# Cross attention with its heads spread between query tiles and output chunks, and one buffer of turned rows

## The reference

```python
def memory_cross_attention(h, m, wq, wkv, wo):
    q = (h @ wq).reshape(b, t, XA_HEADS, XA_HEAD_DIM)          # 4 heads of 256
    k, v = jnp.split(m @ wkv, 2, axis=-1)
    ...
    s = jnp.einsum("bthd,bmhd->bhtm", q, k).astype(jnp.float32) * (XA_HEAD_DIM ** -0.5)
    p = jax.nn.softmax(s, axis=-1).astype(v.dtype)
    o = jnp.einsum("bhtm,bmhd->bthd", p, v).reshape(b, t, D_MODEL)
    return o @ wo

# in each of the two layers l
x = x + memory_cross_attention(rmsnorm(x, norm_xa_g[l]), rmsnorm(mem, norm_mem_g[l]), xa_wq[l], xa_wkv[l], xa_wo[l])
x = x + conv_ffn_2(rmsnorm(x, norm_ffn_g[l]), ...)
```

## Time and profile before

| what | value |
| --- | --- |
| median of 3 runs | 2029.21 us |
| the profiled execution: its time, its span | 2029.21 us, 2027.3 us |
| mean granted TensorE clock | 0.996 |
| PE busy | 1992.5 us, 98% |
| POOL busy | 1444.9 us, 71% |
| DVE, ACT busy | 950.2 us, 614.2 us |
| chain that ended last, PE's share | 95% |
| cross attention of layer 0, from the first query tile to the end of the last output tile | 856.9 to 973.7 us |
| the same of layer 1 | 1537.6 to 1654.3 us |

### The profile page before, as it was taken

How to read it: one execution, slowest core, us unless ns; L and a number is a source line. 1 busy time by engine, 2 the same in 40 slices (tenths; PEclk the granted TensorE clock), 3 DMA queues, 4 the chain that set the end, 5 groups by cost and what they waited for, 6 DMA issues and landing times.

```text
span 2027.3 us, 25594 instructions
## 1 busy us (share of the span) xinstructions
PE 1992.5 (98%) x9432; PEld 1626.1 (80%) x9432; DVE 950.2 (47%) x1567; ACT 614.2 (30%) x1166; POOL 1444.9 (71%) x732
## 2 busy tenths in 40 slices
PE   8999989999999999999999999999999999999997
PEld 6787778888888888788888888877678888888886
DVE  4566444243444897555431422454655553233143
ACT  5554442221014344433210110236732321011011
POOL 7633379777877878874877778687578288777773
PEclk9999999999999999999999999999999999999999
DMA  5741233223223344331332223233013123233221
GB/s 170 138 65 63 81 102 115 94 97 101 94 88 110 104 156 156 104 94 42 96 102 94 95 93 104 76 99 115 1 46 101 42 94 104 94 95 103 94 86 60
DMA packets 57146, 190.79 MB, mean 94 GB/s; under 512 B 6288, under 2 KB 8080, under 8 KB 56944
## 3 DMA queue, kind: packets, MB, share of 16 engines
q1 hardware_dynamic: 52848, 182.71, 29.6%
q10 hardware_dynamic: 4192, 6.58, 1.1%
HBM read 183.50 MB, written 2.10 MB: 92 GB/s over the span
## 4 chain that ended last, share of the span: by engine, by line
PE 95%; DVE 2%; ACT 2%; issue 0%; DMA 0%; SPq 0%; POOL 0%; DVEq 0%; ACTq 0%
PE bank L713 29%; PE bank L715 29%; PE bank L714 29%; PE bank L1368 2%; PE bank L1047 1%; PE bank L958 1%; PE bank L1382 1%; PE bank L1398 1%; ACT EX L1920 1%; PE bank L773 0%; DVE PXL L2659 0%; DMA raw<-weights 0%; PE bank L1069 0%; PE bank L902 0%; DVE EX L2678 0%
## 5 line engine op out<-in xcount | busy, mean ns | idle before, releaser
L609 POOL TENSOR_TENSOR wH<-raw,zero 128x1024 fp32r<-128x1024 f32 (+1 forms) x303 | 577.6, 1906 | 396.0 <-PE bank L715 378.7
L612 POOL TENSOR_TENSOR wL<-raw,wH 128x1024 fp32r<-128x1024 f32 (+1 forms) x303 | 720.7, 2379 | 23.8
L713 PE MATMUL bank<-hnH,wH 128*128 128x512 f32 (+1 forms) x1456 | 575.2, 395 | 14.4 <-POOL wL L603 7.9
L714 PE MATMUL bank<-hnL,wH 128*128 128x512 f32 (+1 forms) x1456 | 569.0, 391 | 0.0
L715 PE MATMUL bank<-hnH,wL 128*128 128x512 f32 (+1 forms) x1456 | 568.9, 391 | 0.0
L713 PEld LDWEIGHTS bank<-hnH,wH 128*128 128x128 f32 (+1 forms) x1456 | 273.7, 188 | 78.4 <-issue 10.0
L714 PEld LDWEIGHTS bank<-hnL,wH 128*128 128x128 f32 (+1 forms) x1456 | 273.9, 188 | 58.4 <-issue 2.1
L715 PEld LDWEIGHTS bank<-hnH,wL 128*128 128x128 f32 (+1 forms) x1456 | 273.7, 188 | 58.5 <-issue 0.7
L713 PE MATMUL bank<-actH,wH 128*128 128x512 f32 x784 | 306.6, 391 | 0.0
L715 PE MATMUL bank<-actH,wL 128*128 128x512 f32 x784 | 305.4, 390 | 0.0
L714 PE MATMUL bank<-actL,wH 128*128 128x512 f32 x752 | 292.9, 390 | 0.0
(11 more groups left out here) (398 smaller groups left out, 2566.6 us busy)
## 6 DMA issues: line engine op xcount, KB each, us to landing
raw<-weights SPq DMA_DIRECT2D x315, 512.0 KB, 3.5
raw<-weights SPq DMA_DIRECT2D x28, 384.0 KB, 3.0
XT<-x_t SPq DMA_DIRECT2D x8, 256.0 KB, 6.4
XT<-x_t ACTq DMA_DIRECT2D x1, 2048.0 KB, 8.3
out<-MIX ACTq DMA_DIRECT2D x8, 256.0 KB, 2.2
maxB<-rowM SPq DMA_DIRECT2D x7, 256.0 KB, 16.5
qkO<-qkA SPq DMA_DIRECT2D x4, 256.0 KB, 4.1
memT<-mem_t ACTq DMA_DIRECT2D x1, 1024.0 KB, 5.6
```

Source lines behind the costliest of these rows:

```text
L609: nc.gpsimd.tensor_tensor(wH[:, slot, 0:w], raw[:, slot, 0:w], nothing.broadcast_to([P, w]), ALU.add)\
L612: nc.gpsimd.tensor_tensor(wL[:, slot, 0:w], raw[:, slot, 0:w], wH[:, slot, 0:w].bitcast(F32), ALU.subtract).then_inc(split, 1)
L713: mm(out_, aH, bH, start=first, stop=False)
L714: mm(out_, aH, bL, start=False, stop=False)
```

## The change

- PE: the attention no longer stands as a block between the two projections. Behind query tile 2 stands scores 0, behind tile 3 turn 0, behind tile 4 scores 1 and values 0, behind tile 5 turn 1, behind tile 6 scores 2 and values 1, behind tile 7 turn 2. Then come output tiles 0 and 1 with chunks 0 and 1; scores 3 and values 2; the same tiles with chunks 2 and 3; turn 3; chunks 4 and 5; values 3; output tile 2 with chunks 0 to 5; tiles 0 to 2 with chunks 6 and 7; tiles 3 to 7 one by one.
- ACT and DVE take their work in the same new order.
- The turned rows have one buffer in place of two, at another address, since the norm's output `hnH`, in whose memory they lay, is now still read. ACT waits for the value product of the head before.
- `OWN_BANKS` now holds banks for the row sum, the query tiles, the attention's tiles and the output tiles, in layer 1 those of layer 0 plus 5. Stages behind it that have no banks there continue from the last of them.

```diff
@@ the table of tiles and banks
-        TILES += [(f"row_sum_x{_i - 1}", 1), (f"xq{_i - 1}", 8), (f"xatt{_i - 1}", 24), (f"xo{_i - 1}", 8)]
+        _q, _a, _o = f"xq{_i - 1}", f"xatt{_i - 1}", f"xo{_i - 1}"
...
+        OWN_BANKS.update({_n: [(_b + (0, 5)[_i - 1]) % 8 for _b in _bs] for _n, _bs in (
+            (f"row_sum_x{_i - 1}", [0]), (_q, [1, 2, 3, 6, 1, 6, 1, 6]),
...
+            (_o, [1, 4, 5, 6, 7, 0, 2, 3]))})
@@ buffers
-        PXH = at("PXH", [P, 2, 2, S], F32R, offset=hn_at)
-        PXL = at("PXL", [P, 2, 2, S], F32R, offset=hn_at + 4 * KB2)
+        PXH = at("PXH", [P, 2, S], F32R, offset=up)
+        PXL = at("PXL", [P, 2, S], F32R, offset=up + 2 * KB2)
@@ PE, cross_attention
-                project(f"xq{l}", hnH, hnL, ready=lambda k: wait_hn(norm, k), lead=2,
-                        after={1: lambda: row_sums(TILE0[f"row_sum_x{l}"], norm)})
...
-                scores(0)
-                for h in range(3):
-                    scores(h + 1)
-                    turn(h)
-                    if h > 0:
-                        values(h - 1)
+
+                def output(tiles, chunks):
+
+                    for k in chunks:
+                        gone_wait(pe, xtile(base, "o", k // 2, k % 2))
+                        for i in tiles:
+                            u, n = POS[f"xo{l}", i], TILE0[f"xo{l}"] + i
+                            if k == 0:
+                                pe.wait_ge(split, u + 1)
+                                claim(n)
+                            cut = slice(k * P, k * P + P)
+                            last = three(psum(n)[:, :], wH[:, u % RING, cut], wL[:, u % RING, cut],
+                                         actH[:, k, :], actL[:, k, :], k == 0, k == KD - 1)
+                            if k == KD - 1:
+                                last.then_inc(unit_done, 1)
+
+                def scores_and_values(h):
+                    scores(h)
+                    values(h - 1)
+                project(f"xq{l}", hnH, hnL, ready=lambda k: wait_hn(norm, k), lead=2,
+                        after={1: lambda: row_sums(TILE0[f"row_sum_x{l}"], norm), 2: lambda: scores(0),
+                               3: lambda: turn(0), 4: lambda: scores_and_values(1), 5: lambda: turn(1),
+                               6: lambda: scores_and_values(2), 7: lambda: turn(2)})
+                output(range(2), range(0, 2))
+                scores_and_values(3)
+                output(range(2), range(2, 4))
                 turn(3)
-                values(2)
+                output(range(2), range(4, 6))
                 values(3)
-                project(f"xo{l}", actH, actL, ready=lambda k: gone_wait(pe, xtile(base, "o", k // 2, k % 2)), lead=2)
+                output(range(2, 3), range(0, 6))
+                output(range(3), range(6, KD))
+                for m in range(3, KD):
+                    output(range(m, m + 1), range(KD))
@@ ACT, rows
-                        if h >= 2:
-                            tile_wait(act, xtile(base, "o", h - 2, 1))
+                        if h >= 1:
+                            tile_wait(act, xtile(base, "o", h - 1, 1))
@@ ACT, the order (exponentials, rows and output_high keep their instructions)
+                for i in range(KD):
+                    query_high(i)
+                    if i in (2, 4, 6):
+                        exponentials(i // 2 - 1)
+                        if i > 2:
+                            output_high(i // 2 - 2)
+                    if i in (3, 5, 7):
+                        rows(i // 2 - 1)
+                exponentials(3)
+                output_high(2)
                 rows(3)
-                output_high(2)
                 output_high(3)
@@ DVE, the order (query, probabilities, rows_low and output_low keep their instructions)
+                for i in range(KD):
+                    query(i)
+                    if i in (2, 4, 6):
+                        probabilities(i // 2 - 1)
+                        if i > 2:
+                            output_low(i // 2 - 2)
+                    if i in (3, 5, 7):
+                        rows_low(i // 2 - 1)
+                memory_part(KD - 1)
+                probabilities(3)
+                output_low(2)
                 rows_low(3)
-                output_low(2)
                 output_low(3)
```

More of the change, by code:

```diff
@@ L181 @@
     if _i > 0:
-        TILES += [(f"row_sum_x{_i - 1}", 1), (f"xq{_i - 1}", 8), (f"xatt{_i - 1}", 24), (f"xo{_i - 1}", 8)]
+        _q, _a, _o = f"xq{_i - 1}", f"xatt{_i - 1}", f"xo{_i - 1}"
+        TILES += [(f"row_sum_x{_i - 1}", 1), (_q, (0, 1, 2)), (_a, (0, 1)), (_q, (3,)), (_a, (2, 3)), (_q, (4,)),
+                  (_a, (4, 5, 6, 7)), (_q, (5,)), (_a, (8, 9)), (_q, (6,)), (_a, (10, 11, 12, 13)), (_q, (7,)),
+                  (_a, (14, 15)), (_o, (0, 1)), (_a, range(16, 24)), (_o, range(2, 8))]
+        OWN_BANKS.update({_n: [(_b + (0, 5)[_i - 1]) % 8 for _b in _bs] for _n, _bs in (
+            (f"row_sum_x{_i - 1}", [0]), (_q, [1, 2, 3, 6, 1, 6, 1, 6]),
+            (_a, [4, 5, 7, 0, 2, 3, 4, 5, 7, 0, 2, 3, 4, 5, 7, 0, 2, 3, 5, 6, 7, 0, 2, 3]),
+            (_o, [1, 4, 5, 6, 7, 0, 2, 3]))})
     TILES += [(f"row_sum_f{_i}", 1)]
@@ L236, in xtile @@
 def xtile(base, kind, h, i):
-    return base + {"s": (0, 2, 6, 12), "t": (4, 8, 14, 18), "o": (10, 16, 20, 22)}[kind][h] + i
+    return base + {"s": (0, 4, 10, 16), "t": (2, 8, 14, 20), "o": (6, 12, 18, 22)}[kind][h] + i
 SCORE_AT = ((0, 3, 0, 0), (1, 2, 0, 1), (1, 0, 3, 2), (2, 1, 0, 3))
@@ L1135, in values @@
                                          VL2[l][:, m, h * 256 + f * P:h * 256 + f * P + P],
-                                         PXH[:, h % 2, m, :], PXL[:, h % 2, m, :], m == 0, m == 1)
+                                         PXH[:, m, :], PXL[:, m, :], m == 0, m == 1)
                         last.then_inc(tile_done, 1)
-                scores(0)
-                for h in range(3):
-                    scores(h + 1)
-                    turn(h)
-                    if h > 0:
-                        values(h - 1)
+                def output(tiles, chunks):
[11 more added lines that the diff above has]
+                                last.then_inc(unit_done, 1)
@@ L1893, in cross_attention, with query_high @@
                         ACT.Copy).then_inc(sig("x_memory_hi"), 1)
-                for i in range(KD):
+                def query_high(i):
                     act.wait_ge(sig("x_q_scaled"), KD * l + i + 1)
@@ L1901, in rows @@
                         tile_wait(act, n)
-                        if h >= 2:
-                            tile_wait(act, xtile(base, "o", h - 2, 1))
-                        run(PXH[:, h % 2, :, pair * MEM:pair * MEM + MEM],
+                        if h >= 1:
+                            tile_wait(act, xtile(base, "o", h - 1, 1))
+                        run(PXH[:, :, pair * MEM:pair * MEM + MEM],
                             psum(n)[:, :].rearrange("p (m q) -> p m q", m=2), ACT.Copy).then_inc(sig("x_rows"), 1)
@@ L1911, in output_high, with exponentials @@
                             .then_inc(sig("x_hi"), 1)
-                for h in range(4):
+                def exponentials(h):
                     for pair in range(2):
@@ L2644, in memory_part, with query @@
                     tt(dst, src, hi.bitcast(F32), ALU.subtract).then_inc(sig("x_memory_low"), 1)
-                for i in range(KD):
+                def query(i):
                     n = TILE0[f"xq{l}"] + i
@@ L2651, in cross_attention @@
                     query_low(i)
-                memory_part(KD - 1)
                 def rows_low(h):
@@ L2657, in rows_low @@
                         dve.wait_ge(sig("x_rows"), 8 * l + 2 * h + pair + 1)
-                        own = (slice(None), h % 2, slice(None), slice(pair * MEM, pair * MEM + MEM))
+                        own = (slice(None), slice(None), slice(pair * MEM, pair * MEM + MEM))
                         free(tt(PXL[own], psum(n)[:, :].rearrange("p (m q) -> p m q", m=2), PXH[own].bitcast(F32),
@@ L2667, in output_low, with probabilities @@
                                 ALU.subtract), n)
-                for h in range(4):
+                def probabilities(h):
                     for pair in range(2):
```

## The result

| what | before | after |
| --- | --- | --- |
| median, in the same job | 2029.42 us (2028.94 to 2029.79) | 2050.53 us (2049.12 to 2052.31) |
| ratio, with 95% interval | | 1.0104 [1.0092, 1.0115] |
| mean granted TensorE clock | 0.996 | 0.990 |

The change makes the kernel 1.04% slower, 21.1 us. The forecast was 12.5 us slower and its range ended at 2048: the sign and the places were right, the size was not. The ratio's interval leaves out 1, so the slowdown is clear of the noise.

A forecast was written before the change was run, and what follows sets the result against it. TensorE (PE) bounds the kernel, busy 1992.5 of 2027.3 us. Waits of 7.28, 4.68 and 5.51 plus 0.5 of handoffs add 18.0, the turns win 5.5: 12.5 us slower, 2041.7, range 2038 to 2048.

The forecast's parts named there:

- The clock: Behind the new PE waits: no loss of granted clock taken, 2.7 to 5.4 us put into the range.
- rival 2: All four new waits lose the clock, 10.8 us more, 2052.5 us; chance 0.05.
- The two waits before scores 0: Each cross-attention layer: PE waits 3.64 us for DVE's last subtraction of query tile 1; 7.3 us in both.
- the chain to 877.78: Ahead of head 0's scores: row sum, root, eight key/value copies, then query work end at 877.78; PE comes at 874.14.
- The seams: Bank neighbours make PE wait 4.68 us at the latent projection, 3.39 and 2.12 at layer 1's first query tiles.
- The turns: Each head's transposes in cross attention: their waits vanish, winning 2.75 us a layer, 5.5 in both.
- Rival 4: Turns still wait because DVE is late with query tiles; none of the 5.5 us won, 2047.2; chance 0.05.
- The last turn: Head 3: 12 output-projection matmuls, 2.7 us, between turn and value product cover 2.1 us of copy and subtractions.
- Weights: Behind the output projection: POOL's weight units arrive in time, nothing taken; upper bound 1 us a layer.
- Rival 3: MLA attention absorbs up to 2.3 us through its waits for DVE's turned rows, 2039.4; chance 0.05.
- rivals 5: Banks at the seams cost nothing, only the attention counts: 2.0 us slower, 2031.2; chance 0.04.
- Rival 6: Head 0's scores find query tiles 0 and 1 ready before 874.14; only the gain is left, 2023.7; chance 0.03.

The follow-up runs named there:

- experiment 4: Kernel before, with bank 0 (the latent tile's) given to the last but one tile of feed-forward 1's last down projection; 2032.42 us, ratio 1.0016.
- experiment 6: Experiment 1's kernel, PE order untouched, ACT copying query tiles 0 and 1 right after the first keys, DVE following; 2024.99 us, ratio 0.9976.
- experiment 3: Kernel before, with bank 0 (the latent tile's) given to the last tile of feed-forward 1's last down projection; 2035.83 us, ratio 1.0036.
- experiment 2: Changed kernel with 66 matmuls added, results unread, where PE stands in the new waits; 2043.16 us, ratio 1.0067.
- experiment 5: Experiment 1's kernel with the attention's heads one query tile later (scores 0 behind tile 3), banks chosen anew; 2024.23 us, ratio 0.9973.
- experiment 1: Changed kernel with other banks at the seams only: layer 1 gets layer 0's banks, output tiles' banks permuted; 2036.48 us, ratio 1.0036.
- experiment 8: Experiment 5's kernel plus 22 matmuls, results unread, in the old 5.57 us wait ahead of feed-forward 0; 2024.59 us, ratio 0.9972.
- experiment 9: Experiment 5's kernel unchanged, run again beside experiment 8 in the same job; 2024.4 us, ratio 0.9973.

## Why the prediction was wrong in size and right in the rest

- **The clock, the step that failed.** "Three of the four waits end well before that, the fourth about there. So I take none". One wait had shown full clock for 4.6 us of its idle time, and I read this as a bound for others. It isn't even one for that wait: in the ten profiles that have it unfilled, always 5.57 us long, the clock fell between 3.3 us (experiments 4 and 6) and 5.2 us (experiment 3) into it. All four new waits lost the clock, for 8.2 us together (experiment 2), against 10.8 for four bounds of 2.7 us. So rival 2, to which I gave 0.05, came true in kind; its 10.8 us were too many because a loss costs 1.4 to 2.45 us here and not 2.7 each time (1.4 us in layer 0, where the clock fell after PE had resumed and came back soonest). With no row on waits of 3 to 5 us, the value between "none" and 2.7 was open for each, and one unknown shared by four waits is one case, not four independent ones: the range had to reach 2052.5. The Trainium skill, "TensorE: Matmul & The Clock Gate", section "Why this matters for your kernels", whose advice against idle gaps the prediction cited and set aside, fits all four places.
- **The two waits before scores 0.** Forecast 3.64 and a handoff of 0.1, measured 3.52 idle in either layer. Right: idle time counts from the shown end of the last matmul; by starts PE came at 874.92 + 0.23 = 875.15 and went on at 878.84, 3.69 us. But "the chain to 877.78 cannot be pulled in" holds only for the order as it stands: experiment 6 pulled it in by 4.1 us with a new order of ACT's copies, and experiment 5 covered it.
- **The seams.** Forecast 4.68; 3.39 and 2.12. Measured 4.64; 3.37 and 1.15. The third is shorter because the three matmuls ahead of it ran at half clock: from 1552.22 to the start of the idle time, 1554.99 - 1.15, are 1.62 us, against 0.68. The two waits with what stood between are 6.14 us against 6.19, since DVE sets the end. Right, and experiments 1, 3 and 4 tie them to the banks.
- **The turns.** 2.75 a layer expected, 2.74 in experiment 5, whose turns stand one place later than in after. Rival 4 (turns still wait) is out.
- **The last turn.** The cover of 2.7 us held: DVE ends the turned rows of head 3 (start 936.93, two of them) about a microsecond before PE comes to them.

```profile
936.93 1.29 DVE L2694 TENSOR_TENSOR PXL<-bank,PXH 128x512 fp32r<-128x512 f32 x2 [2.47 <-ACT PXH L1933]
...
939.30 0.39 PE L720 MATMUL bank<-PXH,actH 128*128 128x512 f32 x1
```

- **Weights.** POOL's seventh unit behind the first output tile starts 28.58 us after the first (28.09 in the earlier trace rows), and PE has no wait for POOL there: nothing, as taken.

```profile
949.16 1.89 POOL L616 TENSOR_TENSOR wH<-raw,zero 128x1024 fp32r<-128x1024 f32 x1 [20.77 <-PE bank L722]
...
977.74 1.89 POOL L616 TENSOR_TENSOR wH<-raw,zero 128x1024 fp32r<-128x1024 f32 x1
```

- **Rival 3** (MLA absorbs) fell with the unchanged PX waits, **rivals 5 and 6** with the waits themselves. Rival 6's time, 2023.7, is nearly what experiments 5 and 6 reach (2024.2 and 2025.0) once its condition is made true.

## What to carry to other kernels

Where banks are numbered by hand, compare the first tiles of a stage with the last of the one before: two such neighbours cost 14 us here, more than the attention's new order could win. A wait of PE must be priced with the matmuls behind it at half clock (1.4 to 2.45 us for the four of after), and as one case for all waits alike. Before you count on winning that back, ask what a faster PE sets off: in experiment 8 it started POOL's splits beside DVE's additions, and that ate the gain. Interleaving pays once each consumer stands behind enough other work to cover the slow engines' queue at that point, or that queue is put in the order of need: with the seams mended, the same idea gave +7 us (experiment 1) and -5 us (experiments 5 and 6).

## What the runs showed of the hardware

- **The clock's fall doesn't follow from a wait's length alone.** Waits of 3.4 to 4.6 us lost it in the three profiles that have one (after, 1 and 3), at different points: 2.3 us into a wait of 3.52 in layer 1 (from 1577.17 - 3.52 = 1573.65 to the edge at 1576), after the end of one of 3.52 in layer 0. A lone wait of 2.32 kept it in one profile, and one of 2.07 with short ones ahead lost it in another.
- **The same program in two executions can differ.** Experiments 5 and 9 are one kernel. Its MLA attention has two waits close together, 1.2 and 1.1 us. In the profile of 5 the clock fell behind them and 16 value matmuls took 4.07 us; in that of 9 it didn't, and they took 2.37. First 5, then 9:

```profile
1488.37 4.07 PE L1427 MATMUL bank<-PX,VL 128*64 128x512 f32 x16 [1.05 <-DVE PX L2874]
...
1489.00:1490.00 1.00, 1.00 (x6) 0.50 0.00 0
```

```profile
1490.25 2.37 PE L1427 MATMUL bank<-PX,VL 128*64 128x512 f32 x16 [1.20 <-DVE PX L2874]
```

  The stretch is 1.7 us longer in 5 (201.99 against 200.29), where the times of that kernel spread by 2.9 to 3.5 us. Other differences between executions are as large: as a whole the profiled execution of 5 was the shorter, 2024.96 against 2025.56 us. The profile of experiment 6 lost the clock at this pair too (3.98 us). What decides it stays open: nothing in the rows of the two profiles tells the waits apart. In the profiles of before and after it was kept, so it plays no part in the difference.
- **DVE's additions slow down beside POOL's splits.** An addition of two SBUF tiles into `ssq` (128x512) took 0.69 us alone and 2.27 to 2.77 us when it started while POOL was splitting weights, in experiment 3 as in 8; in 3 the additions were done 0.9 us before PE needed them and cost nothing.
